# A two-block transformer kernel: the logits of the first and second mixer contract per head over 64 partitions, each head into its own bank

## The reference

```python
# FoX mixer, for each block of 128 queries
logits = einsum('bqhd,bkhd->bhqk', q[:, s0:s1], k[:, :s1]) * scale
logits = logits + c[:, :, s0:s1, None] - c[:, :, None, :s1]      # c: running sum of log_sigmoid(f)
logits = where(tk <= tq, logits, NEG)
outs.append(einsum('bhqk,bkhd->bqhd', softmax(logits), v[:, :s1]))

# NSA mixer, three branches with one query: compressed, selected, window
o = g[..., 0:1] * o_c + g[..., 1:2] * o_s + g[..., 2:3] * o_w
```

## Time and profile before

| | us |
|---|---|
| median of the runs | 1132.73 |
| lowest, highest of 3 | 1129.67, 1133.78 |
| the profiled execution | 1136.28 |
| its span | 1134.5 |

### The profile page before, as it was taken

One profiled execution on the slowest core, in us unless ns is written; L12 is line 12 of the kernel. 1 busy time (PEld: TensorE's weight loads), 2 busy tenths in 40 slices (PEclk: granted clock), 3 DMA queues, 4 the chain that ended last, 5 costly groups with the idle time before them and its releaser, 6 DMA issues. The chain is left out here.

```text
span 1134.5 us, 20621 instructions
## 1 busy us (share of the span) xinstructions
PE 1071.5 (94%) x8304; PEld 1003.0 (88%) x8306; DVE 772.0 (68%) x1276; ACT 542.2 (48%) x862; POOL 75.1 (7%) x60
## 2 busy tenths in 40 slices
PE   7999999998998999899999999998899998999996
PEld 5989889886767999798998999998887898999996
DVE  5665666767784586575556777787677557777785
ACT  5444444455563555443354444545564445444441
POOL 4000013000000400000020000000200320000000
PEclk9899999999998999899899999998999999999999
DMA  8444346771122457201263566664323135656640
GB/s 260 150 136 125 112 149 185 230 230 38 38 76 75 149 153 217 77 1 38 77 184 112 149 186 181 188 185 147 109 80 107 38 112 149 185 166 195 186 155 38
DMA packets 176969, 152.23 MB, mean 134 GB/s; under 512 B 6845, under 2 KB 169220, under 8 KB 176900
## 3 DMA queue, kind: packets, MB, share of 16 engines
q1 hardware_dynamic: 176690, 151.22, 43.9%
q10 hardware_dynamic: 210, 0.05, 0.0%
HBM read 148.12 MB, written 1.05 MB: 131 GB/s over the span
## 5 line engine op out<-in xcount | busy, mean ns | idle before, releaser
L418 PE MATMUL bank<-h_high,w_high 128*128 128x256 f32 x1312 | 385.3, 294 | 12.7 <-DVE w_low L392 5.6
L419 PE MATMUL bank<-h_low,w_high 128*128 128x256 f32 x1312 | 375.4, 286 | 0.0
L420 PE MATMUL bank<-h_high,w_low 128*128 128x256 f32 x1312 | 375.2, 286 | 0.0
L382 ACT ACTIVATE w_high<-ring 128x2048 fp32r<-128x2048 f32 x138 | 262.7, 1905 | 96.4 <-PE bank L420 88.0
L392 DVE TENSOR_TENSOR w_low<-ring,w_high 128x2048 fp32r<-128x2048 f32 x119 | 273.5, 2300 | 25.0 <-ACT w_high L382 23.4
L418 PEld LDWEIGHTS bank<-h_high,w_high 128*128 128x128 f32 x1312 | 255.7, 195 | 23.1 <-issue 10.7
L419 PEld LDWEIGHTS bank<-h_low,w_high 128*128 128x128 f32 x1312 | 255.9, 195 | 0.7 <-issue 0.5
L420 PEld LDWEIGHTS bank<-h_high,w_low 128*128 128x128 f32 x1312 | 255.6, 195 | 0.0
L1024 ACT ACTIVATE ffn_conv<-ffn_normed,par 128x256 f32<-128x256 f32 x88 | 48.1, 594 | 198.1 <-DVE ffn_normed L1037 198.1
L1046 DVE SCALAR_TENSOR_TENSOR ffn_conv<-ffn_normed,par,ffn_conv 128x254 f32<-128x254 f32 (+1 forms) x176 | 77.3, 481 | 65.6 <-ACT ffn_conv L1024 60.5
L418 PE MATMUL bank<-ffn_hidden_high,w_high 128*128 (+1 forms) x352 | 102.2, 290 | 7.1 <-DVE ffn_hidden_low L1070 7.1
(11 more groups left out here) (344 smaller groups left out, 1826.5 us busy)
## 6 DMA issues: line engine op xcount, KB each, us to landing
ring<-in_ffn_w_up_dram SPq DMA_DIRECT2D x44, 1024.0 KB, 6.0
ring<-in_ffn_w_down_dram SPq DMA_DIRECT2D x22, 1024.0 KB, 5.0
ring<-in_fox_w_in_dram SPq DMA_DIRECT2D x16, 1024.0 KB, 5.8
ring<-in_hgrn_w_in_dram SPq DMA_DIRECT2D x16, 1024.0 KB, 5.7
ring<-in_nsa_w_in_dram SPq DMA_DIRECT2D x14, 1024.0 KB, 5.4
ring<-in_fox_w_out_dram SPq DMA_DIRECT2D x4, 1024.0 KB, 5.2
ring<-in_nsa_w_out_dram SPq DMA_DIRECT2D x4, 1024.0 KB, 5.2
ring<-in_hgrn_w_out_dram SPq DMA_DIRECT2D x4, 1024.0 KB, 5.3
```

What stands on the lines that cost most here:

```text
L382: i = nc.scalar.activation(dst, src, ACT.Copy)
L418: nc.tensor.matmul(o, ah, bh, start=start, stop=False, **kw)
L419: nc.tensor.matmul(o, ah, bl, start=False, stop=False, **kw)
L420: return nc.tensor.matmul(o, al, bh, start=False, stop=stop, **kw)
```

## The change

For the first two mixers (`halves=True`; the MLA mixer keeps the old form) a pair unit's logits become two float32 matmuls of w columns. Head e takes the 64 partitions of its own half of the queries and of the keys, and writes to bank 2 + e. Unit u uses columns (u % 2) * 256 onward in both banks, so units u (even) and u + 1 share the two banks. They enter together: TensorE issues `logits(k)` and `logits(k+1)` in step k for even k, after the exponential of unit k-1; VectorE issues both `smallest` there, after both logits; and both exponentials wait for both `smallest`. The row and mask matmuls still contract over 128 partitions, now head by head: a mask matmul of 128 columns for each head in place of one of 256. Blocks units keep their form, and enter in pairs too. The eight banks become slices of one tensor.

```diff
+            def bank(self, u):
+                if self.halves and "blocks" not in unit:
+                    return banks[:, 2:4, u % 2 * S:u % 2 * S + unit["w"]]
             def logits(self, pe, u):
-                if u >= 2:
+                if self.halves and u % 2 == 0 and u:
+                    pe.wait_ge(a_exped, self.u0 + u)
+                elif not self.halves and u >= 2:
                     pe.wait_ge(a_exped, self.u0 + u - 1)
+                if self.halves and "blocks" not in unit:
+                    (q, k), = unit["qk"]
+                    mask, c0 = unit["mask"]
+                    for e in range(2):
+                        half = slice(e * HD, (e + 1) * HD)
+                        nc.tensor.matmul(o[:, e, :], q[half], k[half, e, :], start=True, stop=False, ...)
+                    for e in range(2):
+                        for pick, row in unit.get("rows", ())[e:e + 1]:
+                            nc.tensor.matmul(o[:, e, :], pick, row, start=False, stop=False, ...)
+                        mm = nc.tensor.matmul(o[:, e, c0:c0 + P], ident_bf[:, :], mask, start=False, stop=True, ...)
+                    mm.then_inc(a_multiplied, 1)
+                    return
             def smallest(self, dve, u):
-                dve.wait_ge(a_multiplied, self.u0 + u + 1)
+                dve.wait_ge(a_multiplied, self.u0 + (min(u // 2 * 2 + 2, self.n) if self.halves else u + 1))
             def exp(self, act, u):
-                act.wait_ge(a_least, self.u0 + u + 1)
+                act.wait_ge(a_least, self.u0 + (min(u // 2 * 2 + 2, self.n) if self.halves else u + 1))
+            def entering(self, k):
+                if self.halves:
+                    return (k, k + 1) if k < self.n and k % 2 == 0 else ()
+                return (k,) if k < self.n else ()
             def pe_step(self, pe, k):
-                if k < self.n:
-                    self.logits(pe, k)
+                for u in self.entering(k):
+                    self.logits(pe, u)
             def dve_step(self, dve, k):
-                if k < self.n:
-                    self.smallest(dve, k)
+                for u in self.entering(k):
+                    self.smallest(dve, u)
```

More of the change, by code:

```diff
@@ L146, in sem @@
             return ctx.enter_context(nc.semaphore(name))
-        B = [ctx.enter_context(nc.psum_tensor(f"bank{i}", [P, 512], F32)) for i in range(8)]
+        banks = ctx.enter_context(nc.psum_tensor("bank", [P, 8, 512], F32))
+        B = [banks[:, i, :] for i in range(8)]
         x = sb("x", [P, DC, S])
@@ L654, in build, with __init__ @@
         class Attention:
-            def __init__(self, area, units, groups, take, blocks=None):
+            def __init__(self, area, units, groups, take, blocks=None, halves=False):
+                self.halves = halves
                 self.units, self.groups, self.take = units, groups, take
@@ L697, in logits @@
                 unit = self.units[u]
-                if u >= 2:
+                if self.halves and u % 2 == 0 and u:
+                    pe.wait_ge(a_exped, self.u0 + u)
+                elif not self.halves and u >= 2:
                     pe.wait_ge(a_exped, self.u0 + u - 1)
                 o = self.bank(u)
+                if self.halves and "blocks" not in unit:
[3 more added lines that the diff above has]
+                        half = slice(e * HD, (e + 1) * HD)
+                        nc.tensor.matmul(o[:, e, :], q[half], k[half, e, :], start=True, stop=False,
+                                         skip_group_check=True)
+                    for e in range(2):
+                        for pick, row in unit.get("rows", ())[e:e + 1]:
+                            nc.tensor.matmul(o[:, e, :], pick, row, start=False, stop=False, skip_group_check=True)
+                        mm = nc.tensor.matmul(o[:, e, c0:c0 + P], ident_bf[:, :], mask, start=False, stop=True,
+                                              skip_group_check=True)
+                    mm.then_inc(a_multiplied, 1)
+                    return
                 if "blocks" in unit:
@@ L1335, in build @@
                     v=lambda e, kt, c=c: v[:, kt, (2 * c + e) * HD:(2 * c + e + 1) * HD]))
-        att = Attention(area, units, DC, lambda g, ps: nc.vector.tensor_copy(oT[:, g, :], ps))
+        att = Attention(area, units, DC, lambda g, ps: nc.vector.tensor_copy(oT[:, g, :], ps), halves=True)
         out_pe, out_dve, out_act, out_pool = project_out(T["fox_out"], nrm_nsa, (o_hi, o_lo),
@@ L1625, in build @@
         att2 = Attention(att_area, units, DC, lambda g, ps, oT=oT: nc.vector.tensor_copy(oT[:, g, :], ps),
-                         blocks=(bw, bt))
+                         blocks=(bw, bt), halves=True)
         FIRST = NT2["q2"]
```

## The result

The changed kernel takes 1153.45 us (median; 1151.49 to 1163.74) against 1131.89 us before: 1.0202 of the time before, 95% interval 1.0144 to 1.0261. The forecast was 1153, from 1136 to 1168. In a second series of six runs, beside 17 runs of the kernel before, it was 1154.53 us, 1.0207 (1.0152 to 1.0261).

What follows compares the result with a forecast made beforehand. TensorE's stream was taken as the bound, busy 94% of the span. Terms -5.2 + 9.6 + 1.0 + 14.6 = +20.0 us on the runs' median of 1132.7 gave about 1153 us, range 1136 to 1168.

Steps and rivals of the forecast that it cites:

- the terms of form: Logits and mask matmuls on TensorE: overlap -5.2, changes between 64 and 128 rows +9.6, extra mask instruction +1 us.
- the waits: TensorE waiting on the reduction, exponential and copy chains once pairs enter together, mostly in NSA's attention: +14.6 us.
- Part 1: Float32 logits matmuls: partial overlap of the heads saves 0.215 us per w = 256 unit, none for w = 128; -5.2 us.
- The mark that I had set: First logits matmul to first mask matmul, w = 256: 0.65 us plus change of form; 0.86 without overlap, 0.43 with all.
- side by side: Rival, logits matmuls: both heads run wholly together, -15.5 us, so +9.7 in all, 1142 us; chance 0.13.
- Part 2: TensorE going from 128 to 64 rows and back: 96 more changes of form at 0.10 us each, +9.6 us.
- Parts 1 to 3: Logits overlap -5.2, changes of form +9.6, one more small mask matmul with its load +1 us: +5.4 together.
- neighbours only: Logits matmuls: only head 1's first instruction may overlap head 0's second, making three terms of four; -5.2 us.
- Part 4: Pairs entering together: exponentials wait for both reductions, delaying copies and entries; NSA +9.9 and +4.7, FoX 0, total +14.6 us.
- its cover failing: FoX: projection matmuls and the step itself hide the chain to the weighing; failing by 0.3 us a pair costs +2.4.
- absorbed: Rival: present waits and work before them take up the longer chains in attention; +5.4 us, 1138; chance 0.13.
- faster: Rival: full overlap, present waits (4.1 us) gone, changes of form free; -18.6 us, 1114; needs form under 0.05 us; chance 0.10.

Runs made afterwards that it cites:

- pair_only: Changed kernel with pairs still entering together, but with the matmuls of the kernel before (128 partitions, both heads in one bank): 1158.01 us, 1.0234 of the time before.

## Why the prediction was right, step by step

The time was right (1153 against 1153.45), and that it was right to half a microsecond is luck: the terms of form, which I had at 5.4 us, measure about 0, and the clock, which I had at nothing, gives 6 to 7. The largest term, the waits, was right.

**Part 1** (-5.2 us) failed in its mechanism. I let only neighbours overlap, "the first of head 1 may run beside the second of head 0". The heads run wholly side by side, 0.007 us apart. The mark that I had set for a w = 256 unit was 0.65 us plus the change of form, so 0.75, and 0.43 plus the same, 0.53, if all overlapped; 0.64 lies midway. It looks like the three terms of 0.215, and is two of 0.215 with 0.1 more at each. By streaming alone the overlap is worth the -15.5 of the rival "side by side".

**Part 2** (+9.6 us) had the right price for a change of form (0.15 - 0.055 = 0.1 going in) and put a second 0.1 on the way back, where the trace has 0.1 behind each of the two terms over 64 rows. Per unit that is three times 0.1, 0.29 us, for 0.43 (w = 256) or 0.215 (w = 128) saved. A FoX pair: 0.645 saved, 0.58 paid, and the timeline has 0.05 us more in four pairs. Parts 1 to 3 were to be +5.4 us; pair_only against the changed kernel says about 0 by the medians (1.0234 and 1.0207, the intervals overlap) and -2.4 at equal clock. The rule of the Trainium skill, TensorEngine Tiling (Array Packing), section Key Properties, agrees in both halves with what this trace shows: tiles that work in parallel (0.007 us apart) and something lost at a change of mode (0.1 us going in). With the order of starts it is not so plain. The Trainium skill, TensorE: Matmul & The Clock Gate, section The mechanism, has it that matmuls start and end strictly in order. The kernel issues head by head, and yet a first term of each head starts (47.863 and 47.870) before a second term of either (48.183), so my step from that rule to "neighbours only" failed. Whether TensorE or the compiled stream puts the terms in this order the trace doesn't tell.

**Part 4** (+14.6 us) was right in mechanism and in most places. NSA's waits went up by 12.3 us, for 14.6: {12,13} waits 1.52 for 1.6, {17,18} 1.21 and 1.51 in two pieces for 2.2, {25,26} 2.15 for 2.1, {27,28} 1.66 for 1.9, {30,31} and {34,35} 1.5 each for 1.7, {4,5} 1.95 for 2.7, and {21,22} nothing for 0.6. The wait of 1.44 at {15,16} is gone, as forecast. (The places with an even step first add to 6.8 + 3.1, not 6.5 + 3.4; the 9.9 is right.) FoX, which I had at 0, pays 2.3 us, what I had named as the price of its cover failing (2.4), so that 12.3 + 2.3 comes to my 14.6 by luck: `exp` of unit 1 now holds the second pair by 0.76, and the last weighings wait 1.30, since they drain two to a place. Here I took the trace's 0.31 us between the exponential's end and the start of step 2 for a margin, and it was less than none.

**What I hadn't at all** is the clock. NSA's stretch grew by 23.1 us, of which waits explain 12.3. The rest, 10.8, fits the clock of 0.90 there (0.10 x 135.6 = 13.6 us at most), and pair_only, whose matmuls are those of before, has the same (22.1, 11.9 of it waits). But that is the clock of one stretch in one pair of profiles, and this pair got it back behind NSA, so it can't be added to the program's time. For that the executions serve: the mean clock is 0.979 over the 62 of before and 0.972 over the 11 of the changed kernel, which by 10 us per 0.01 is 6 to 7 us, and at equal clock the changed kernel lies 14.7 us above before. That the idle causes the lower clock is not shown.

In sum: forecast -5.2 + 9.6 + 1.0 + 14.6 = 20.0. Found: form about 0, waits 12.3 + 2.3 = 14.6 for the 14.7 us at equal clock, and 6 to 7 of clock, 21 together; 21.6 us by the medians, 21.4 in the second series. The rival "absorbed" fell in pair_only, "faster" with its own point: a change of form costs 0.1, not under 0.05. "Side by side" was right about the hardware and wrong about the time, as the 0.1 at each term and at each change takes what it gives.

## What to carry to other kernels

When two units are made to share a buffer, the engines behind it get their work in twos: look in each engine's queue for what stands behind the second of them, here a copy for which TensorE waits; moving that copy ahead of the exponential was worth 1% on the kernel before, more than the new matmuls could give. Running two heads side by side over 64 rows each took as long as one, and still gained little: 0.64 us for 0.86 with 256 columns, nothing with 128 (0.43 both), and 0.1 for going in. So count what a change of form costs before halving a contraction, most of all with short moving operands. Where a mark of the forecast is nearly met, check the parts of the number too. And where executions come with their clock, compare kernels at the same clock: that told 15 us of kernel from 6 of clock here.

## What the runs showed of the hardware

- Two float32 matmuls over rows 0 to 63 and 64 to 127 into two banks start 7 ns apart and take together what one of them takes alone, 0.63 to 0.64 us for 256 columns in two terms.
- Over 64 rows a float32 term of 256 columns follows the one before after 0.32 us; over 128 rows after 0.215.
- With 18.5 us of waits in pieces of up to 2.3 us, for 6.2 before, TensorE's clock was at the lower of its levels for about a fifth of 250 to 350 us, where before it was never. In the same two profiles it was higher behind NSA than before, 0.99 for 0.97.
- An execution's span follows its mean granted clock: 10 us for 0.01 in the kernel before, over 62 executions from 0.972 to 0.990, none more than 1.8 us off the line.
